# Moving the root-mean-square step behind the last operand, and the set-up and state-space blocks earlier, in a two-layer trunk on one core

## The reference

```python
for i in range(DEPTH):
    h = _rms_norm(x, norm_mix[i])
    if i % N_MIXERS == 0:
        x = x + _gmlp_mixer(h, gm_w_in[j], gm_ln_g[j], gm_ln_b[j], gm_w_s[j], gm_b_s[j], gm_w_out[j])
    else:
        x = x + _s5_mixer(h, s5_w_in[j], s5_a_re[j], ..., s5_d[j], s5_w_out[j])
    x = x + _swiglu(_rms_norm(x, norm_ffn[i]), ffn_w1[i], ffn_w3[i], ffn_w2[i])
    gate = jax.nn.sigmoid(_rms_norm(x, norm_ple[i]) @ ple_w_gate[i])
    x = x + gate * (p[i] @ ple_w_proj[i])
return _rms_norm(x, norm_final)
```

## Time and profile before

| | |
|---|---|
| median of three runs | 2257.13 us (2255.93, 2257.33, 2257.13) |
| the profiled execution's own time | 2255.93 us |
| its span, first to last instruction | 2254.0 us |
| mean granted TensorE clock | 0.999 of full speed |
| PE busy | 2238.2 us, 99% of the span |
| DVE busy | 1440.8 us, 64% |
| ACT busy | 1022.7 us, 45% |
| POOL busy | 495.5 us, 22% |

### The profile page before, as it was taken

The page is one execution under the profiler, slowest core; times in us unless marked ns, Lnnn a source line. Parts: engine busy times, 40 slices in busy tenths (PEclk is TensorE's granted clock), DMA queues, the critical chain, the costliest instruction groups (busy, mean ns, idle before and its releaser), DMA issues.

```text
span 2254.0 us, 28581 instructions
## 1 busy us (share of the span) xinstructions
PE 2238.2 (99%) x11378; PEld 1843.4 (82%) x11378; DVE 1440.8 (64%) x1579; ACT 1022.7 (45%) x1241; POOL 495.5 (22%) x469
## 2 busy tenths in 40 slices
PE   9999999999999999999999999999999999999998
PEld 7888888888888888888878888888888888888886
DVE  7878767667766766666667866555555445555665
ACT  5544454444444444445444354444444344444444
POOL 1245325455665544301002100000000000000001
PEclk9999999999999999999999999999999999999999
DMA  8667788888887888887789867677766667767764
GB/s 289 194 198 231 228 243 266 241 249 254 251 243 221 255 263 240 247 260 266 236 244 331 309 207 231 201 217 222 215 214 209 194 194 221 220 213 230 228 214 141
DMA packets 347838, 525.81 MB, mean 233 GB/s; under 512 B 105929, under 2 KB 125273, under 8 KB 347193
## 3 DMA queue, kind: packets, MB, share of 16 engines
q1 hardware_dynamic: 336784, 488.50, 71.1%
q0 software_dynamic: 8320, 30.75, 3.7%
q10 hardware_dynamic: 2600, 4.74, 0.6%
HBM read 473.05 MB, written 50.86 MB: 232 GB/s over the span
## 4 chain that ended last, share of the span: by engine, by line
PE 94%; DVE 3%; DMA 3%; issue 0%; ACT 0%; SPq 0%; ACTq 0%; DVEq 0%
PE PS L1553 60%; PE PS L1559 30%; DVE WLO L1059 1%; PE PS L1764 1%; DMA HT<-zd 1%; DMA ROOTU<-rootd 1%; DMA RAW<-in_ple_w_gate 1%; PE PS L1673 0%; PE PS L1584 0%; DMA X<-in_x 0%; PE PS L1789 0%; DMA rootd<-ROOT 0%; PE PS L1781 0%; DVE Z L1340 0%; PE PS L1842 0%
## 5 line engine op out<-in xcount | busy, mean ns | idle before, releaser
L1553 PE MATMUL PS<-WHI,OP 128*128 128x512 f32 x6208 | 1540.7, 390 | 0.1
L1059 DVE TENSOR_TENSOR WLO<-RAW,WHI 128x1024 fp32r<-128x1024 f32 x783 | 1027.9, 1324 | 655.8 <-ACT WHI L767 652.3
L1553 PEld LDWEIGHTS PS<-WHI,OP 128*128 128x128 f32 x6208 | 1160.8, 188 | 245.4 <-issue 4.6
L767 ACT ACTIVATE WHI<-RAW 128x1024 fp32r<-128x1024 f32 x783 | 825.5, 1061 | 939.6 <-PE PS L1559 811.1
L1559 PE MATMUL PS<-WLO,OP 128*128 128x512 f32 x3104 | 830.4, 389 | 2.1 <-DVE WLO L1059 1.9
L1559 PEld LDWEIGHTS PS<-WLO,OP 128*128 128x128 f32 x3104 | 582.2, 188 | 125.1 <-DVE WLO L1059 4.1
L751 POOL TENSOR_TENSOR ON<-X,GF 128x1024 f32<-128x1024 f32 x3 | 9.9, 3297 | 945.1 <-DVE X L1395 945.1
L654 POOL TENSOR_TENSOR TA<-BRAW,FAC 128x64 f32<-128x64 f32 x16 | 9.8, 613 | 317.2 <-DMA BRAW<-in_s_b_im 317.2
L1071 DVE TENSOR_TENSOR OP<-HT,OP 128x512 fp32r<-128x512 f32 x50 | 34.6, 733 | 55.3 <-ACT OP L782 55.3
L782 ACT ACTIVATE OP<-HT 128x512 fp32r<-128x512 f32 x50 | 28.9, 625 | 74.5 <-DMA HT<-zd 74.5
L815 ACT ACTIVATE S<-PS,RC 128x512 f32<-128x512 f32 x66 | 41.7, 683 | 30.7 <-PE PS L1559 30.7
(11 more groups left out here) (213 smaller groups left out, 959.9 us busy)
## 6 DMA issues: line engine op xcount, KB each, us to landing
RAW<-in_ffn_w SPq DMA_DIRECT2D x528, 512.0 KB, 4.6
RAW<-in_gm_w_in SPq DMA_DIRECT2D x64, 512.0 KB, 4.9
RAW<-in_ple_w_gate SPq DMA_DIRECT2D x64, 512.0 KB, 4.9
RAW<-in_s_w_out SPq DMA_DIRECT2D x64, 512.0 KB, 5.1
zd<-ZT SPq DMA_DIRECT2D x37, 512.0 KB, 3.7
HT<-zd SPq DMA_DIRECT2D x148, 128.0 KB, 5.7
RAW<-in_gm_w_out SPq DMA_DIRECT2D x32, 512.0 KB, 4.9
RAW<-in_s_w_in SPq DMA_DIRECT2D x32, 512.0 KB, 5.6
```

Of the source, the lines that this page charges most:

```text
L767: A_.activation(hi_of(t), RAW[:, t % RING, :], ACT.Copy).then_inc(hi_ready, 1)
L1059: V_.tensor_tensor(lo_of(t), RAW[:, t % RING, :], hi_of(t).bitcast(F32), ALU.subtract).then_inc(lo_ready, 1)
L1553: T_.matmul(dst[:, th, :], x_part, WHI[:, slot, f], start=first and kk == 0 and part == 0, stop=False)
```

## The change

Three sets of numbers are lowered, and the norm's step at the end of `gate0` is moved: on DVE, `moments()` goes from before the last operand's low part to behind it, and on ACT `root(i)` goes from before the last operand's high part to behind it and behind two more weight tiles. The store to `rootd` follows it, with one more weight tile between the store and the wait for it.

```diff
-quads("us", range(NT), 16, None, 2)
+quads("us", range(NT), 16, None, 1)
@@
-SET_AT = start("v", 1) + 2
+SET_AT = start("v", 1)
@@
-INTO_AT = [W0 + 8 * (d // 2) + 16 + d % 2 for d in range(DUOS)]
-OUT_AT = [W0 + 8 * (d // 2) + 20 + 2 * (d % 2) for d in range(DUOS - 2)] + [W0 + 44, W0 + 46]
+INTO_AT = [W0 + 8 * (d // 2) + 14 + d % 2 for d in range(DUOS)]
+OUT_AT = [W0 + 8 * (d // 2) + 18 + 2 * (d % 2) for d in range(DUOS - 2)] + [W0 + 42, W0 + 43]
@@
-TQ_AT += [(W0 + g, W0 + g + 1) for g in (17, 19, 25, 27, 33, 35)]
+TQ_AT += [(W0 + g, W0 + g + 1) for g in (15, 17, 23, 25, 31, 33)]
...
@@
-            def gates(stage, i):
+            def gates(stage, i, last=True):
                 for n in range(NT):
                     until(end(stage, n))
                     take(stage, n, in_s, ACT.Sigmoid)
-                    if n == NT - 1:
-                        until(end(stage, n) + 2)
-                        root(i)
-                        act.wait_ge(root_ready, i + 1)
-                        for h in range(2):
-                            act.dma_start(rootd[h].unsqueeze(1), ROOT[:, h:h + 1]).then_inc(root_out, 16)
-                    quad_of(stage, n, 2)
+                    if last:
+                        quad_of(stage, n, 2)
+                if last:
+                    until(end(stage, NT - 1) + 5)
+                    root(i)
@@
-            until(end("gate0", NT - 1) + 5)
+            act.wait_ge(root_ready, RMS["win"] + 1)
+            for h in range(2):
+                act.dma_start(rootd[h].unsqueeze(1), ROOT[:, h:h + 1]).then_inc(root_out, 16)
+            until(end("gate0", NT - 1) + 6)
             act.wait_ge(root_out, 32)
@@
                     gated(stage, n, PS[:, 6:8, :])
-                    if n == NT - 1:
-                        moments()
                     quad_of(stage, n, 2)
+                moments()
```

More of the change, by code:

```diff
@@ L183 @@
 TE_AT = [G0 + 12, G0 + 26]
-TQ_AT += [(W0 + g, W0 + g + 1) for g in (17, 19, 25, 27, 33, 35)]
-TD_AT += [(W0 + g, W0 + g + 1) for g in (21, 29, 31, 37, 39)]
-TK_AT += [(W0 + g, W0 + g + 1) for g in (23, 31, 33, 39, 41)]
-TE_AT += [W0 + g for g in (20, 21, 28, 29, 36, 37)]
+TQ_AT += [(W0 + g, W0 + g + 1) for g in (15, 17, 23, 25, 31, 33)]
+TD_AT += [(W0 + g, W0 + g + 1) for g in (19, 27, 29, 35, 37)]
+TK_AT += [(W0 + g, W0 + g + 1) for g in (21, 29, 31, 37, 39)]
+TE_AT += [W0 + g for g in (18, 19, 26, 27, 34, 35)]
 def set_before(d):
```

## The result

| | before | after |
|---|---|---|
| median of four runs each, taken together | 2256.53 us (2255.67 to 2257.33) | 2282.77 us (2281.97 to 2284.14) |
| profiled execution (its span) | 2255.93 (2254.0) us | 2284.6 (2282.2) us |
| mean granted TensorE clock | 0.999 | 0.993 |

The ratio is 1.0117 with an interval of 1.0100 to 1.0135. The medians lie 26.2 us apart, the two profiled spans 28.2. The forecast was 2271.0 (2264 to 2278). The sign was right, the size was not: half the loss was missing.

The account below looks back on a forecast made before the run. PE, busy 99% of the span with a row of weight tiles, was taken as the bound. Terms 2.9 + 1.5 + 4.9 + 3.6 + 1.0 = 13.9 us on 2255.93 gave 2269.8, by the median 2271.0; range 2264 to 2278.

Parts of the forecast that it names:

- Term 1: At `set_up`, placed two tiles earlier, PE waits for DVE's copy into `AN`: +2.9 us.
- Term 2: At the last `us` transpose, placed one tile earlier, PE waits for Z from DVE: +1.5 us (1.3 to 1.8).
- Term 4: At the first `into_states`, placed two tiles earlier, PE waits for `UP`: +3.6 us (2.5 to 4.7).
- 5. The other loads of `UP`: Second to fourth column: ACT issues the loads later against the tiles, the block wants them earlier; +1.0 us in all (0 to 5).
- at nothing: Term for POOL's table loads, whose queue order is unchanged, and `out_of_states`, which moves with `into_states`: no cost.
- Rival B: Clock falls to 1.2 GHz after the waits of terms 3 and 4, one tile each: +5.4, 2276.4 us; chance 0.08.
- Term 3: Mean squares behind the operand: root stored 8.5 us later, store and load taking 9 us each; +4.9 us, floor 0.8.
- A: Root's store and load again take 8.59 and 12.62 us, making term 3 8.5: 2274.6 us; chance 0.22.
- C: `ROOTU` loads almost unhindered; term 3 is 0.8 and term 5 nothing: 2265.9 us; chance 0.16.
- D: Root's DRAM trip shrinks to 10.8 us or less in a quieter stretch; no slowdown that can be told, 2260.2 us; chance 0.06.
- the 2258 us beside the fixed cost: Estimate by the skill's 2.0 us fixed DMA cost: terms 3 and 4 about -2 together, sum 2.3; given rival D's chance.

Follow-up runs that it names:

- the state-space part alone: Kernel before with only `INTO_AT`, `OUT_AT`, `TQ_AT`, `TD_AT`, `TK_AT` and `TE_AT` changed (`into_states`, `out_of_states` and their table loads two tiles earlier): 2278.37 us, ratio 1.0101.
- The `U_AT` experiment: The state-space part alone plus `U_AT` lowered by one, so the way to `UP` comes one tile earlier: 2260.21 us, ratio 1.0018 to the kernel before.
- The experiment with late tables: The state-space part alone, but POOL's loads of `TD` and `TK` in `win` keep their old tiles: 2270.58 us, ratio 1.0064 to the kernel before.
- the experiment on ACT: The state-space part alone, with ACT taking up the load of `UP` one tile sooner: 2273.78 us, ratio 1.0078 to the kernel before.
- the second experiment: Kernel before with only the edits of `gates`, `root` and `moments`, moving the mean squares behind the operand: 2254.88 us, ratio 0.9994.
- the last one: The second experiment plus ACT's wait for the store, DVE's reciprocal and ACT's take of column 0 one tile later each: 2253.48 us, ratio 0.9990 to the kernel before.
- the whole change with `UT` earlier: The changed kernel with `U_AT` lowered by one, so the way to `UP` comes one tile earlier: 2265.04 us, ratio 1.0039 to the kernel before.

## Why the prediction was wrong

**What held.** The way of reading: a block set ahead of its input makes PE stand still, and time lost is not won back (PE's lag stays where it is from 1305 us to the end). Term 1: 2.81 us for `AN` against 2.9. Term 2: 1.48 for Z against 1.5. Term 4: 3.33 for the first `UP` against 3.6.

Term 4 is in part luck. It supposed that the reciprocal and PE would be late by the same amount. The reciprocal came 3.9 us later than before (1159.12 against 1155.19) and PE 5.3 us (tile 410 at 1171.28 against 1165.94), which takes 1.4 off the wait; the way from the reciprocal to the last `UP` took 18.2 instead of 17.2 us, which puts 1.0 back. With the state-space part alone the same wait is 1.87 us, outside the 2.5 to 4.7 given.

**The failed step: "5. The other loads of `UP`".** It said +1.0, at most 5; it measured 12.0 us of waits (2.34 + 5.72 + 3.95) and 4.8 of slow clock behind them, 16.8. Two things in it were wrong:

- *Who releases the loads.* I took the load of `UP` to be ready at ACT's turn and counted what stands ahead of it in ACT's queue, 4.3 us. What it waits for is `UT` by way of `ud`, and `UT` had moved behind two scans in DVE's queue. I had set ACT's order before and after side by side and never DVE's at the same place, although the edit changes that one in the same way. The `U_AT` experiment shows it: 18 of the 21.7 us are back.
- *How long the loads take.* I let them take what they took, near 5.5 us. The loads of the tables that move with the blocks meet them, and they take 7.3 to 8.0 at the median. I had put the table loads "at nothing" because their order on POOL is unchanged. Their order is, but not what they run beside. The experiment with late tables shows it: 7.8 us less.

**Rival B, the clock, at 0.08.** It was not a rival but a part of every long wait. Behind the 2.81 us before `set_up` the granted clock is still 1.00 up to 40 us, then 0.71 and 0.50 in the next two microseconds, and the tile there costs 1.6 us more; behind the four waits for `UP` it is 2.9, 1.5, 1.7 and 1.6. That makes 9.3 us in all, against 5.4 in the rival, which gave it to two places and not to `set_up`. I argued "no row of before shows that level". No row of before has a wait of more than 1.6 us on PE after the start either (the longest of all is 2.4 us for `IDENT`, at the start), so the rows could not speak against it. The Trainium skill (TensorE: Matmul & The Clock Gate, "HAM oscillation — how this bites in real kernels") warned that matmuls behind waits for DMAs come back at the low level; by that rule the sum wanted such a tail at each of the four waits for `UP`, and the trace agrees at all four. The waits in the Trainium skill's example there are of about 3 to 5 us; here one of 2.34 was enough. Of the three waits for other engines one, the 2.81 us for `AN`, has such a tail too.

**Term 3, the mean squares: 4.9 forecast, about 0.2 measured.** The chain of waits in the changed kernel, beside the earlier trace rows (start, length, what):

```profile
1145.06 0.36 ACTq L949
1145.45 9.15 DMA rootd<-ROOT
...
1155.78 3.32 DMA ROOTU<-rootd
...
1159.12 0.18 DVE RC L1485
```

The store was issued at 1145.06 ("about 1145") and took 9.5 us from its first issue to its landing ("9"). The load took 3.32, where I had 9. The rows had given 12.62 for one such load and 5.8 for a weight load; I chose nearer the former. In the four profiles with the later store it takes 3.3, 4.3, 4.9 and 6.7 us; in the ten with the old place 11.3 to 14.6. PE waits 2.14 us for the high part of 405 instead of 1.63 for the low part of 406, with no fall of the clock here. The floor of the term, 0.8, was set by that very wait and was the better guess.

The prediction had held a rule against these sizes. The Trainium skill (DMA: Bandwidth & Descriptors, "Anatomy of one DMA") gives its fixed cost of about 2.0 us for DMAs that GpSimd issues. These two are issued by ACT, and with 9.15 and 3.32 us the trace disagrees still.

**The other rivals.** A, the trip at its old cost, is refuted: 14.1 us from the first issue of the store to the reciprocal, not 22.8. C had the load right and the total wrong, since it put term 5 at nothing. D wanted a trip of at most 10.8 us, and no run has that. Two of the sums beside them were off: D's 3.1 leaves out the 1.0 of term 5, and the 2258 us beside the fixed cost adds its 2.3 to the profiled execution (2255.93); added to the median of 2257.13, as in the forecast, it is 2259.4.

**The sum, mended**, to the two profiled spans (28.2 us). The first half comes to 5.1 us, by PE's position at the end of `gate0` (2.81 + 1.6 + 1.48 = 5.9, less 0.4 of an earlier start and small waits of before that are gone); the root 0.2; the first `into_states` 3.3 + 2.9; the other three 12.0 + 4.8. Together 28.3. Against the forecast's 13.9 that is 15.8 more in term 5, 2.6 more at the first `into_states`, 0.7 more in the first half and 4.7 less at the root: 14.4 more.

**What stays open.** Why the loads of `UP` land sooner in the experiment on ACT. What decides whether the clock falls behind a wait near 2 us. And what held the load of `ROOTU` for 12.6 us in the kernel before. The rows point at POOL's 512 KB load of `TK`: it was issued at 1142.74, 0.2 us behind that load (1142.54), and the DMA engines were 0.86 busy until it landed; in the changed kernel it is issued at 1147.80, 8.0 us ahead of the load (1155.78), and their share is 0.40. In the second experiment and the last one the shares are 0.60 and 0.77, and the load takes 4.9 and 6.7 us. But a share alone doesn't set the time, and no run moved that table load by itself, so this is likely and not shown.

## What to carry to other kernels

When a block is moved in a hand-written order, follow its input back to the engine that makes it and look at that engine's queue before and after; a turn on the issuing queue says nothing if the data come later. Count transfers that move along with a block as new neighbours of those that stay, even where their own order is the same. And price a wait on TensorE of about 2 us or more, in a kernel that never stands still, at its length plus 1.3 to 3 us for the clock behind it, if it falls. Other matmuls in the wait kept the clock up at its place here, but the total fell in only one of the two experiments on it, and not clearly.

## What the hardware showed that was not expected

- The clock's fall is not a matter of the wait's length alone near 2 us. Behind 2.14 us in the changed kernel the next tile ran at full level (2.12 us), behind 2.06 us at the same place, in the whole change with `UT` earlier, it took 3.66. After the start of the program no wait up to 1.76 us was followed by a fall in these rows, and every wait of 2.79 and more was. In between, 1.87 us was enough before the first `into_states` of the state-space part alone, and 2.38 us was not at tile 406 in the experiment on ACT:

```profile
1157.13 1.19 PE L1559 MATMUL PS<-WLO,OP 128*128 128x512 f32 x4 [2.38 <-DVE WLO L1059]
1158.25 2.14 PE L1553 MATMUL PS<-WHI,OP 128*128 128x512 f32 x8
```

- Matmuls whose result nobody reads keep the clock up: 26 transposes for 2.9 us, and the window from 36 to 44 us stays at 1.00, where it was 0.50 to 0.59 from 38 to 44 without them.
- A load of 0.5 KB took between 3.3 and 14.6 us over the versions of this program, and the store ahead of it, of the same size, 7.4 to 10.8.
